# A mixture-of-experts step: from gathered expert rows to rows added into one sum per token

## The reference

```python
top_val, top_idx = lax.top_k(logits, TOP_K)          # 4 of 32 experts
top_w = jax.nn.softmax(top_val, axis=-1)
...
def expert_block(args):                              # blocks of up to 128 rows, one expert each
    e, toks = args
    gu = x_pad[toks] @ w_gu[e] + b_gu[e]
    ...
    return act @ w_down[e] + b_down[e]
outs = lax.map(expert_block, ...)
y = jnp.zeros((n_tok + 1, D), jnp.float32).at[slot_tok].add(outs.reshape(-1, D) * slot_w[:, None])
x = x + gt2 * y
```

## Time and profile before

| what | us |
|---|---|
| median of three runs | 2030.82 |
| profiled execution, whole | 2033.37 |
| its span | 2031.5 |
| PE busy, DVE busy, ACT busy, POOL busy | 1772.7, 1490.1, 1025.0, 143.8 |
| first expert DMA of POOL to last expert store | 800.46 to 1969.0 |
| combine, first DMA to the end | 1975.13 to 2031.5 |

### The profile page before, as it was taken

One profiled execution on the slowest core, in us unless ns is written; L12 is line 12 of the kernel. 1 busy time (PEld: TensorE's weight loads), 2 busy tenths in 40 slices (PEclk: granted clock), 3 DMA queues, 4 the chain that ended last, 5 costly groups with the idle time before them and its releaser, 6 DMA issues. The chain is left out here.

```text
span 2031.5 us, 27856 instructions
## 1 busy us (share of the span) xinstructions
PE 1772.7 (87%) x10263; PEld 1305.2 (64%) x10263; DVE 1490.1 (73%) x1337; ACT 1025.0 (50%) x885; POOL 143.8 (7%) x144
## 2 busy tenths in 40 slices
PE   3399999975597794999999999999999999999960
PEld 0044567643594343788888788888878888888850
DVE  0165344446765344899999999999999999999955
ACT  1011222222231231777777777777777777777731
POOL 0000000000500110010000000000000000000006
PEclk8689999957798895999999999999999999999985
DMA  9840311510000517899999999999999999999736
GB/s 381 328 144 33 99 47 48 219 48 27 22 5 5 191 63 272 306 380 377 385 372 396 380 378 384 377 384 374 395 383 376 383 375 395 369 391 382 300 131 236
DMA packets 116777, 535.24 MB, mean 263 GB/s; under 512 B 14553, under 2 KB 16899, under 8 KB 82634
## 3 DMA queue, kind: packets, MB, share of 16 engines
q1 hardware_dynamic: 102512, 491.01, 62.4%
q0 software_dynamic: 7040, 25.30, 3.3%
q10 hardware_dynamic: 7162, 18.05, 2.2%
HBM read 498.42 MB, written 35.86 MB: 263 GB/s over the span
## 5 line engine op out<-in xcount | busy, mean ns | idle before, releaser
L1939 DVE TENSOR_TENSOR ex_weights_lo<-weight_ring,ex_weights_hi 128x2048 fp32r<-128x2048 f32 x256 | 574.3, 2285 | 3.9 <-ACT ex_weights_hi L1874 1.2
L1874 ACT CAST ex_weights_hi<-weight_ring 128x2048 fp32r<-128x2048 f32 x256 | 486.5, 1914 | 147.0 <-PE banks L2048 91.7
L2027 PE MATMUL banks<-ex_weights_hi,ex_rows_hi_lo 128*128 128x512 f32 x2048 | 516.2, 394 | 3.0 <-ACT ex_weights_hi L1874 3.0
L2027 PEld LDWEIGHTS banks<-ex_weights_hi,ex_rows_hi_lo 128*128 128x128 f32 x2048 | 381.7, 189 | 87.5 <-issue 6.8
L1944 DVE TENSOR_TENSOR ex_weights_lo<-weight_ring,ex_weights_hi 128x2048 fp32r<-128x2048 f32 x128 | 293.1, 2294 | 52.7 <-ACT ex_weights_hi L1881 52.6
L1881 ACT CAST ex_weights_hi<-weight_ring 128x2048 fp32r<-128x2048 f32 x128 | 244.6, 1914 | 101.2 <-PE banks L2027 101.2
L2027 PE MATMUL banks<-ex_weights_lo,ex_rows_hi_lo 128*128 128x512 f32 x1024 | 276.0, 392 | 0.0
L2048 PE MATMUL banks<-ex_weights_hi,ex_rows_hi_lo 128*128 128x512 f32 x1024 | 258.4, 395 | 2.6 <-ACT ex_weights_hi L1881 2.6
L2048 PEld LDWEIGHTS banks<-ex_weights_hi,ex_rows_hi_lo 128*128 128x128 f32 x1024 | 190.4, 188 | 54.8 <-issue 13.2
L2027 PEld LDWEIGHTS banks<-ex_weights_lo,ex_rows_hi_lo 128*128 128x128 f32 x1024 | 193.4, 189 | 41.0 <-DVE ex_weights_lo L1939 0.2
L2048 PE MATMUL banks<-ex_weights_lo,ex_rows_hi_lo 128*128 128x512 f32 x512 | 137.3, 390 | 0.0
(11 more groups left out here) (331 smaller groups left out, 1742.3 us busy)
## 6 DMA issues: line engine op xcount, KB each, us to landing
weight_ring<-in_moe_w_gu SPq DMA_DIRECT2D x256, 1024.0 KB, 10.1
weight_ring<-in_moe_w_down SPq DMA_DIRECT2D x128, 1024.0 KB, 9.9
weight_ring<-in_w_ada SPq DMA_DIRECT2D x8, 3072.0 KB, 30.5
expert_rows<-ex_plain ACTq DMA_DIRECT2D x32, 512.0 KB
weight_ring<-in_w_in SPq DMA_DIRECT2D x6, 2048.0 KB, 20.7
expert_rows<-arena SPq DMA_DIRECT2D x16, 512.0 KB
weight_ring<-in_cache_k SPq DMA_DIRECT2D x24, 256.0 KB, 3.3
weight_ring<-in_cache_v SPq DMA_DIRECT2D x24, 256.0 KB, 3.8
```

Source lines behind the costliest of these rows:

```text
L1874: nc.scalar.copy(hi_of(i), raw_chunk(m, i)).then_inc(q["gu_hi"], 1)
L1939: V.tensor_sub(lo_of(i), raw_chunk(m, i), plain(hi_of(i))).then_inc(q["gu_lo"], 1)
L2027: last = T.matmul(m.bank[n], x[:, i, :], w[:, n * 512:(n + 1) * 512], start=False, stop=(i == GU - 1 and w is lo))
```

## The change

Every block's rows are scaled and added straight to their tokens' rows in DRAM, `token_sums`, 520 token rows and 128 spare ones for padding lanes.

- attention: SP clears these 648 rows with 6 DMAs in place of 16.
- mix_and_route: `blk_hot` has 96 columns in place of 49, half of them token numbers (counted from 1) and half weights; DVE has one more multiplication of 960 elements a partition. PE's 20 products are 96 columns wide. ACT copies `slot_weight`, and then DVE works out `gather_idx` and `sum_idx` in 7 small linked instructions. The integer copy of `slots` is gone.
- experts: ACT copies the block's weight column and scales by it while it copies `y` out of PSUM. The plain store is gone. POOL copies the block's column of `sum_idx` and issues an indirect DMA from `y` to `token_sums` with `compute_op=ALU.add`, in the loop behind the next gather, and waits before it for the add before (`y_out`). One add of a zeroed `y` goes out before the first gather.
- combine: the 20 gathers, the scaling and the additions are gone. SP loads the five tiles of sums, ACT the gate rows and the x2 tiles; DVE multiplies and adds, SP stores.

```diff
--- before.py
+++ after.py
@@ -511,10 +511,11 @@
                 cache_rows(io["cache_v"], m.v_new, vg[:, b % 4], b, vg_in[b % 4])
                 if b == 3:
                     sp.wait_ge(zero_set, 1)
-                    for j in range(EXPERTS, BLOCKS):
-                        sp.dma_start(m.y_dram[j * BLK:(j + 1) * BLK, :], zero_rows).then_inc(rows_zero, 16)
+                    for j in range(NT + 2):
+                        r = min(P, ROWS - j * P)
+                        sp.dma_start(m.sum_dram[j * P:j * P + r, :], zero_rows[0:r, :]).then_inc(rows_zero, 16)
             sp.wait_ge(m.out_v, 16 * (NT + 1))
-            sp.wait_ge(rows_zero, 16 * MORE)
+            sp.wait_ge(rows_zero, 16 * (NT + 2))
 
...
@@ -1454,18 +1456,19 @@
...
-        blk_hot = a.take((NT + 1) * TOPK, BLOCKS + 1)
+        blk_hot = a.take((NT + 1) * TOPK, 2 * BLOCKS)
...
             act.wait_ge(q["idx_mm"], 1)
-            nc.scalar.copy(m.gather_idx[:, :], m.bank[0][:, 0:BLOCKS + 1])
+            nc.scalar.copy(m.slot_weight[:, :], m.bank[0][:, BLOCKS:2 * BLOCKS]).then_inc(q["idx_done"], 1)
 
...
-            V.tensor_copy(m.slots[:, :], slotf)
             link(V.tensor_scalar(lane_of, slotf, 1.0 / BLK, 1.0 / (2 * BLK) - 0.5, ALU.mult, ALU.add))
...
-            link(V.tensor_tensor(blk_hot, along(blk_of, BLOCKS + 1), each(blk_no, pairs), ALU.is_equal))
-            V.tensor_mul(blk_hot.rearrange("p (t c) b -> p t (c b)", c=TOPK), blk_hot.rearrange("p (t c) b -> p t (c b)", c=TOPK),
-                         along(tok_of, TOPK * (BLOCKS + 1))).then_inc(q["blk_ready"], 1)
+            by_token, by_weight = blk_hot[:, :, 0:BLOCKS], blk_hot[:, :, BLOCKS:2 * BLOCKS]
+            link(V.tensor_tensor(by_weight, along(blk_of, BLOCKS), each(blk_no, pairs), ALU.is_equal))
+            link(V.tensor_tensor(by_token.rearrange("p (t c) b -> p t c b", c=TOPK), by_weight.rearrange("p (t c) b -> p t c b", c=TOPK),
+                                 tok_of.unsqueeze(2).unsqueeze(3).broadcast_to([P, NT + 1, TOPK, BLOCKS]), ALU.mult))
+            V.tensor_mul(by_weight, by_weight, along(m.weights[:, :], BLOCKS)).then_inc(q["blk_ready"], 1)
...
             link(V.tensor_copy(m.more_expert[:, MORE:MORE + 1], over[:, 2, EXPERTS - 1:EXPERTS]))
+            dve.wait_ge(q["idx_mm"], 1)
+            dve.wait_ge(q["idx_done"], 1)
+            found = m.bank[0][:, 0:BLOCKS]
+            link(V.tensor_scalar(ocmp_f, found, -1.0, 0.0, ALU.add, ALU.max))
+            link(V.tensor_copy(m.gather_idx[:, :], ocmp_f))
+            link(V.tensor_scalar(ocmp_f, found, 0.0, tok_of[:, NT:NT + 1], ALU.is_equal, ALU.mult))
+            link(V.tensor_scalar(slot_f, found, 0.0, float(NB), ALU.is_equal, ALU.mult))
+            link(V.tensor_add(slot_f, slot_f, ocmp_f))
+            link(V.scalar_tensor_tensor(slot_f, found, -1.0, slot_f, ALU.add, ALU.add))
+            link(V.tensor_copy(m.sum_idx[:, :], slot_f))
 
...
-                    last = T.matmul(m.bank[0][:, 0:BLOCKS + 1], lane_hot[0:r, i, :], blk_hot[0:r, i, :],
+                    last = T.matmul(m.bank[0][:, 0:2 * BLOCKS], lane_hot[0:r, i, :], blk_hot[0:r, i, :],
...
@@ -1856,11 +1872,31 @@
                 nc.gpsimd.indirect_dma_start(out=xg, out_offset=None, in_=m.h2_dram,
                                              in_offset=bass.IndirectOffsetOnAxis(ap=idx, axis=0)).then_inc(q["xg_in"], 16)
 
+            def add(index_copy, n):
+                index_copy.then_inc(q["sum_idx_copied"], 1)
+                pool.wait_ge(q["sum_idx_copied"], n)
+                nc.gpsimd.tensor_tensor(turn, turn, turn, ALU.mult)
+                nc.gpsimd.indirect_dma_start(out=m.sum_dram, out_offset=bass.IndirectOffsetOnAxis(ap=sum_idx, axis=0), in_=y,
+                                             in_offset=None, compute_op=ALU.add).then_inc(q["y_out"], 16)
+
+            def add_rows(b):
+
+                pool.wait_ge(q["y_out"], 16 * (b + 1))
+                pool.wait_ge(q["y_copied"], b + 2)
+                add(nc.gpsimd.tensor_copy(sum_idx, m.sum_idx[:, bass.ds(b, 1)]), b + 2)
+
             def body(b, prev, ahead, further):
                 if ahead:
                     gather(b + 1)
-
-            all_blocks(pool, lambda b, further: gather(b), body, lambda b: None)
+                if prev:
+                    add_rows(b - 1)
+
+            def last(b):
+                add_rows(b)
+                pool.wait_ge(q["y_out"], 16 * (b + 2))
+
+            add(nc.gpsimd.tensor_copy(sum_idx, m.sum_idx[:, 0:1]), 1)
+            all_blocks(pool, lambda b, further: gather(b), body, last)
 
...
             def rows_out(b):
                 act.wait_ge(q["y_out"], 16 * (b + 1))
+                nc.scalar.copy(weight, m.slot_weight[:, bass.ds(b, 1)]).then_inc(q["weight_copied"], 1)
+                act.wait_ge(q["weight_copied"], b + 1)
                 act.wait_ge(q["dn_used"], DN * (b + 3))
-                nc.scalar.copy(y, m.psum[:, 2 * D:3 * D]).then_inc(q["y_copied"], 1)
-                act.wait_ge(q["y_copied"], b + 2)
-                act.dma_start(m.y_dram[bass.ds(b * BLK, BLK), :], y).then_inc(q["y_out"], 16)
+                nc.scalar.activation(y, m.psum[:, 2 * D:3 * D], ACT.Copy, scale=weight).then_inc(q["y_copied"], 1)
 
...
-                act.wait_ge(q["y_out"], 16 * (b + 2))
-
-            act.wait_ge(q["ones_set"], 3)
-            act.dma_start(m.y_dram[0:1, :], y[0:1, :]).then_inc(q["y_out"], 16)
+
             all_blocks(act, first, body, last)
...
+        total = a.take(NT + 1, D)
...
         @block.sync
         def _(sp):
-            row = m.mod_dram[NB:NB + 1, 5 * D:6 * D]
-            sp.dma_start(row_p, row.broadcast_to([P, D])).then_inc(row_in, 16)
-            sp.dma_start(row_s, m.mod_dram[0:NB, 5 * D:6 * D]).then_inc(row_in, 16)
-            sp.wait_ge(added, 1)
             for t in range(NT + 1):
                 r = rows_of(t)
-                sp.dma_start(x2[0:r, t, :], m.x2_dram[t * P:t * P + r, :]).then_inc(x2_in, 16)
+                sp.dma_start(total[0:r, t, :], m.sum_dram[t * P:t * P + r, :]).then_inc(total_in[t], 16)
             for t in range(NT + 1):
                 r = rows_of(t)
-                sp.wait_ge(total, t + 1)
+                sp.wait_ge(summed, t + 1)
                 dst = io["y_prompt"][0, t * P:(t + 1) * P, :] if t < NT else io["y_sample"][:, 0, :]
-                sp.dma_start(dst, x2[0:r, t, :]).then_inc(out, 16)
+                sp.dma_start(dst, total[0:r, t, :]).then_inc(out, 16)
             sp.wait_ge(out, 16 * (NT + 1))
-
-        @block.gpsimd
-        def _(pool):
-            def add_x2(t):
...
-                nc.gpsimd.tensor_tensor(x2[0:r, t, :], x2[0:r, t, :], acc[0:r, t % 2, :], ALU.add).then_inc(total, 1)
-
-            for i in range((NT + 1) * TOPK):
-                r = rows_of(i // TOPK)
-                before, c = (i - 8) // TOPK, (i - 8) % TOPK
-                if i >= 8 and c == 0:
-                    pool.wait_ge(scaled, before + 1)
-                elif i >= 8:
-                    pool.wait_ge(added, (TOPK - 1) * before + c)
-                nc.gpsimd.indirect_dma_start(out=ring[0:r, i % 8, :], out_offset=None, in_=m.y_dram,
-                                             in_offset=bass.IndirectOffsetOnAxis(ap=m.slots[0:r, i:i + 1], axis=0))\
-                    .then_inc(got[i % 8], 16)
-                if i >= 8 and c == TOPK - 1:
-                    add_x2(before)
-            add_x2(NT - 1)
-            add_x2(NT)
 
...
+            row = m.mod_dram[NB:NB + 1, 5 * D:6 * D]
+            act.dma_start(row_p, row.broadcast_to([P, D])).then_inc(row_in, 16)
+            act.dma_start(row_s, m.mod_dram[0:NB, 5 * D:6 * D]).then_inc(row_in, 16)
             for t in range(NT + 1):
                 r = rows_of(t)
-                i = t * TOPK
-                act.wait_ge(got[i % 8], 16 * (i // 8 + 1))
-                if t >= 2:
-                    act.wait_ge(total, t - 1)
-                nc.scalar.activation(acc[0:r, t % 2, :], ring[0:r, i % 8, :], ACT.Copy, scale=m.weights[0:r, i:i + 1])\
-                    .then_inc(scaled, 1)
+                act.dma_start(x2[0:r, t, :], m.x2_dram[t * P:t * P + r, :]).then_inc(x2_in[t], 16)
...
+            dve.wait_ge(row_in, 32)
             for t in range(NT + 1):
                 r = rows_of(t)
-                sum_ = acc[0:r, t % 2, :]
-                dve.wait_ge(scaled, t + 1)
-                for c in range(1, TOPK):
-                    i = t * TOPK + c
-                    dve.wait_ge(got[i % 8], 16 * (i // 8 + 1))
-                    if c > 1:
-                        dve.wait_ge(added, (TOPK - 1) * t + c - 1)
-                    nc.vector.scalar_tensor_tensor(sum_, ring[0:r, i % 8, :], m.weights[0:r, i:i + 1], sum_, ALU.mult, ALU.add)\
-                        .then_inc(added, 1)
-                dve.wait_ge(added, (TOPK - 1) * (t + 1))
-                if t == 0:
-                    dve.wait_ge(row_in, 32)
```

(27 more changed lines are left out.)

17 lines of the change are left out of this document (7 added, 10 removed).

## The result

The changed kernel takes 2074.03 us (median of 4 runs, 2071.30 to 2077.29), the kernel before on the same chip 2030.9 us. The ratio is 1.0217, with a 95% interval of 1.0197 to 1.0236: the change costs 2.2%, about 44 us, where the prediction had a gain of 24. The profiled execution has a span of 2075.5 us, 44.0 more than before.

A forecast was written before the change was run, and what follows sets the result against it. PE was taken to set the loop's pace, 35.75 us a pass. Terms summed as -33.9 (combine) + 5.0 (start) + 4.5 (end of experts) = -24.4 us, so a median of 2006.4 us, range 1997 to 2034.

The forecast's parts named there:

- The loop, POOL: In experts' loop the gather moves behind the add and lands at 1361.5, PE wanting it at 1366.8: cost 0.
- rival 2: In the loop the add is slow in its own queue, so the gather comes late: +99 us, 2105; chance 0.06.
- Rival 1: In 31 loop passes the add saturates the DMA engines; at three times the assumed occupancy +98 us, 2104; chance 0.14.
- The loop, DMA: In the loop the add's extra DMA work lowers idle time from 2.8 to 1.5 us a pass: cost 0.
- A: Occupancy of the DMA engines by one add in the loop: 2.6 us, between 1.3 and 14.4; PE waits from 4.6.
- the reserve: In the loop, time in hand between a weight load's landing and ACT's first read of it: 14.7 us.
- The loop, ACT: In the loop the weight copy and scaled copy put 0.4 us ahead of a split that waits anyway: cost 0.
- Mix_and_route: The stage ends 2.7 us later, wider products costing 0; with the zero add, experts' start is 5.0 us later.
- The end of experts: From the last store, now an add, to combine's start: 7.3 us for about 2.9, +4.5 us, between 2 and 8.
- Combine: The last stage takes 22.5 us for 56.4, between 18.5 and 27: a gain of 33.9 us.
- Attention: SP issues 10 DMAs less, but waits 17.4 us for PE right behind them: 0.
- the upper bound of the parts: Slow end of the summed stage estimates for the whole kernel, given as 2017 us; the fast end was 1998.

The follow-up runs named there:

- the early index: The changed kernel with POOL's copy of the sum_idx column ahead of its wait for `y`, order of add and gather kept: 2008.29 us, ratio 0.9880.
- the halves: The changed kernel with each DVE subtraction of 2048 columns done as two of 1024, POOL's code untouched: 2014.47 us, ratio 0.9902.
- the gathers first: The changed kernel with the gather for block b + 2 ahead of the add of block b - 1 on POOL: 2015.64 us, ratio 0.9900.
- the one with no adds: The kernel before the change, with POOL made to wait for `y` of the block before ahead of its gather: 2033.30 us, ratio 0.9987.
- Plain scatters: The changed kernel with accumulation left out of the indirect DMA, so rows are overwritten, order kept: 2012.79 us, ratio 0.9890.
- Two adds: The kernel that issues gathers ahead of adds, with each add done again into a second tensor: 2024.21 us, ratio 0.9962.

## Why the prediction was wrong, step by step

**The loop, POOL** is the step that failed, and it carries 65 of the error of 68 us. It put the add's DMA 1.0 us and the gather's 3.1 us behind `y`; the trace shows 3.3 and 11.2, or 9.0 in the other pass. The rest of the step held, in part by luck. The landing was taken as 7.4 + 4 = 11.4 us and is 10.6, but the 4 was put there for the add in front, and with no add it is 10.8. The time from `y` to PE's want was 19.8 and is 19.9 (1341.68 to 1361.63). 19.9 - 11.2 - 10.6 = -1.9, and PE waited 1.99. The 5.3 us in hand were all spent by four small instructions and the issue of the add. Their durations came from the place in the pass at which the earlier trace rows shows them, 1332 us, where DVE has gaps between its instructions (busy 2.52 of 3 us). Even there the copy's 0.54 us was in part a wait: with DVE idle it takes 0.18. At the new place DVE is full, 3.00 of 3.00. I took a moved instruction to last as long as where it was. The rows that warned of it were cited in the prediction.

The Trainium skill states the rule, and I didn't weigh it: *SBUF — State Buffer*, section Who interferes with whom, says that a DVE instruction with two inputs in SBUF contends with a GpSimd instruction that reads SBUF, that their shared ports are an exclusive lock, and that the order of issue decides who waits. The trace agrees: 0.19 us alone, 2.12 beside DVE's 2.29, 1.06 beside its 1.22. The same section infers that generating a DMA's descriptors is not held up by such a DVE instruction; here the issue of the indirect gather went from 1.01 to 2.87 us beside it, and that of the add became shorter with DVE's instructions, so for an indirect DMA the measurement decides against it.

**The size of a wait.** The wait itself is only half of the loss. What I called 3.3 us a pass in rival 2 was a wait alone; the trace shows that in 12 of the 15 long passes the granted clock then goes to its lower level (1.2 GHz) for a while, and the loss is 33 us of waits and 66 of time. In return it comes only in every other pass. In the pass that waits `y` is ready 1.4 us into a subtraction of DVE, in the other about at the start of one; why the two take turns no run isolated.

**Rival 2** had the right symptom, PE's transposes waiting for the gather while the DMA share falls (0.97 to 0.92), and the wrong cause. Rows in front of the gather in its queue would have shown in the landing, and that is 10.6 us with accumulating adds, 11.1 with plain ones and 10.8 with none. It isn't excluded for an add that stands nearer: in the kernels with the early index and with the halves the add is issued only 4.7 and 3.7 us ahead of the gather, and there the gather lands 11.8 and 11.6 us after an issue of only 1.0, so some 10.7 us behind the issue's end, where it is 7.9 with no add. Which part of this is the add's no run isolated; PE didn't wait. **Rival 1** didn't come about.

**The loop, DMA.** A, the occupancy of an add, was taken as 2.6 us. The queue of POOL took 10.9% of the span's engine time in the kernel with the gathers first and 3.6% in the one with no adds; over 1070 us and 29 adds, 0.073 x 1070 / 29 = 2.7 us. Plain scatters give (6.9 - 3.6)% and 1.2 us. So the rows of an add do overlap, as the prediction had it, against 14.4 us for rows one after another. Two adds, 5.4 us, lie beyond the 4.6 where PE was to begin waiting, and it did. The same sum would have had a loss of 31 x (5.4 - 2.8 - 1.3) - 14.7 = 25.6 us there, and it was 8.4. The copies of `y` tell which term was off: once the reserve is used up a pass is longer by 0.8 us, not by 1.3, and 14.7 us at 0.8 a pass last for 18 passes, about the 17 (and the two ahead of them) that stayed at 35.77. So the 14.7 of reserve was right, and the idle time was put 0.5 us too small, or the two adds take 0.5 less.

**The loop, ACT**: 0, and right: ACT's waits go on naming PE (L1910 on L2081, 127.0 us in 87 waits).

**Mix_and_route** and the start: +3.6 for +5.0. The 40 products took 8.13 us with 96 columns and 8.90 with 49. A part of the 8.13 ran at the upper clock, but in 6.90 us wholly at 0.50 there were 32 products in 6.84 us, 0.214 each for 0.2225 before, so the width costs nothing, as said. The first gather's DMA starts 3.7 us later (800.46 and 804.16), and so do the transposes: nothing was given back, and nothing lost, by the loads beside it.

**The end of experts**: +8.5 for +4.5. The chain of 0.8 us on POOL was right. The last add was taken to be done 6.3 us after its issue, and it landed after 6.5: that was right too. But combine starts 13.7 after the issue. A plain scatter takes 10.5 (1979.82 to 1990.35) and landed after 3.3, so 7.2 us come behind the landing in both, and the accumulate costs 3.2, all of it in the landing. Of the 7.2 us, 5.4 are POOL's DRAIN at the end of the stage (5372 ns from 2046.2 on), and this is the term that the prediction didn't have. In the kernel before, POOL's DRAIN took 8.1 us as well, but from 1870.2 on, a hundred us ahead of the stage's end, as POOL had no work left; there ACT's store was last, whose own DRAIN took 0.07, and combine began 6.1 us after its issue. The change makes POOL the last engine of the stage.

**Combine**: 23.1 us for 22.5, right. **Attention**: nothing moved, right.

**The sum.** The kernel with the early index is at 0.988 of the kernel before (0.9857 to 0.9903), and 0.988 is what 2006.4 to 2030.8 would have been; its span is 2006.0 us for 2007.1. So with the failed step put right the sum holds, but that it fits so well is luck: its first transposes came at 808.34, no later than before, where +5.0 was forecast, and its end of experts is 15.2 us long, 8 more than before where +4.5 was. And the upper bound of the parts is 2030.8 - 29.4 + 9 + 8 = 2018, not 2017.

## What to carry to other kernels

When an instruction is moved, take its duration from a row at its new place, beside what runs there, and not from its old place; for POOL that means looking at which DVE instructions with two SBUF inputs lie there, as a one-element copy can cost a whole one of them. Ask too which engine ends a stage last: POOL's DRAIN there cost 5.4 us. Of a queue that serves both something urgent and something that isn't, the urgent one is issued first, and all that doesn't depend on the late operand (here an index copy of 0.7 us) is done ahead of the wait. Price a wait of PE in such a loop at more than its length: here 15 waits of some 2 us cost twice their sum.

## What the runs showed of the hardware

- An indirect DMA's issue on POOL is stretched by DVE as POOL's own arithmetic is: 2.87 us where a subtraction of DVE is running, 1.01 where the issue starts 0.02 ahead of one (1341.92 and 1341.94 in the kernel with the gathers first). The accumulating one takes 1.58 with DVE idle, 3.50 beside subtractions of 2.29 us and 2.43 beside their halves of 1.22.
- An accumulating indirect DMA of 128 rows of 4 KB takes the 16 DMA engines 2.7 us beside loads, 2.2 times the plain one's 1.2.
- Alone on the DMA engines, an accumulating indirect DMA of 128 rows of 4 KB lands 6.5 us after its issue, a plain one 3.3.
- At the end of a stage POOL's DRAIN takes 5.4 us behind an indirect DMA that has landed. From the last issue to the next stage's first DMA it is 13.7 us with the add, 10.5 with the plain scatter, and 6.1 with ACT's plain store.
- A wait of 2 us on PE was followed by a stretch of 5.2 us at a mean granted clock of 0.67; 12 of 15 such waits (2.0 to 2.6 us) were followed by a fall of the clock, and 3 of 2.1 to 2.3 us were not.
